# Two transformer blocks on one core: squares summed on GpSimd, a feed-forward that multiplies raw tokens, and first iterations walked by feature tile

## What is computed

```python
def rms_norm(x, g):
    y = xf * lax.rsqrt(jnp.mean(xf * xf, axis=-1, keepdims=True) + EPS)
    return y * g
def modulate(h, shift, scale):
    return h * (1.0 + scale) + shift
mod_x = silu(c) @ w_ada + b_ada                  # six vectors of 1024: shifts, scales, gates
x = x + gt_m * rms_norm(mix_x, g_post_mix)
fx = swiglu(modulate(rms_norm(x, g_pre_ffn), sh_f, sc_f), w_ffn_in, w_ffn_out)   # gu0, dn0
x = x + gt_f * rms_norm(fx, g_post_ffn)
...
h = h + 0.5 * swiglu_2(rmsnorm(h, ffn1_norm), w_gate, w_up, w_down)              # gu1, dn1
u = rmsnorm(h, mix_norm)                                                         # in2k, in2g, ...
h = h + mixed @ w_out                                                            # wout2
h = h + 0.5 * swiglu_2(rmsnorm(h, ffn2_norm), w_gate, w_up, w_down)              # gu2, dn2
return rmsnorm(h, final_norm)
```

## Time and profile before

| | |
|---|---|
| median of 3 runs | 1073.89 us (1072.05 to 1074.85) |
| profiled execution: its own time | 1075.8 us |
| profiled execution: span | 1074.0 us |
| mean granted TensorE clock | 0.97 |
| busy: TensorE, VectorE, ScalarE, GpSimd | 1016.3, 601.5, 529.1, 51.1 us |

### The profile page before, as it was taken

The page is one execution under the profiler, slowest core; times in us unless marked ns, Lnnn a source line. Parts: engine busy times, 40 slices in busy tenths (PEclk is TensorE's granted clock), DMA queues, the critical chain, the costliest instruction groups (busy, mean ns, idle before and its releaser), DMA issues.

```text
span 1074.0 us, 19630 instructions
## 1 busy us (share of the span) xinstructions
PE 1016.3 (95%) x7693; PEld 927.5 (86%) x7693; DVE 601.5 (56%) x902; ACT 529.1 (49%) x787; POOL 51.1 (5%) x73
## 2 busy tenths in 40 slices
PE   5788999997999999989999999999999999999996
PEld 0466566785999999979999999999888899999996
DVE  2643574657555554375555544665586766566653
ACT  3253345645555654355555433553554665655440
POOL 0021110001000000000000000200120000000000
PEclk9799999898999999989999999999899999999998
DMA  8676343134756587416556763653233356666741
GB/s 316 199 254 203 122 166 110 40 119 156 235 179 195 173 220 211 137 59 194 159 184 186 202 172 99 204 160 115 65 114 120 129 184 183 188 187 200 214 142 39
DMA packets 189438, 175.39 MB, mean 163 GB/s; under 512 B 7344, under 2 KB 178624, under 8 KB 189008
## 3 DMA queue, kind: packets, MB, share of 16 engines
q1 hardware_dynamic: 183744, 153.24, 46.7%
q0 software_dynamic: 4928, 17.51, 4.8%
q10 hardware_dynamic: 720, 4.02, 1.0%
HBM read 173.67 MB, written 1.05 MB: 163 GB/s over the span
## 4 chain that ended last, share of the span: by engine, by line
PE 87%; DVE 4%; DMA 4%; ACT 2%; issue 1%; POOL 0%; DVEq 0%; SPq 0%; ACTq 0%
PE acc L1695 23%; PE acc L1696 23%; PE acc L1697 23%; PE wk L1739 2%; DMA raw<-in_w_ada 2%; DMA stage<-in_w_ada 2%; PE acc L2039 2%; PE wk L2085 1%; PE wk L1766 1%; PE acc L1846 1%; PE acc L1848 1%; PE acc L1847 1%; PE wk L1911 1%; PE wk L2278 1%; PE wk L1897 1%
## 5 line engine op out<-in xcount | busy, mean ns | idle before, releaser
L993 DVE TENSOR_TENSOR lo<-raw,hi 128x1024 fp32r<-128x1024 f32 (+1 forms) x260 | 330.0, 1285 | 252.7 <-ACT hi L509 252.3
L1695 PE MATMUL acc<-nH,hi 128*128 128x256 f32 (+2 forms) x1400 | 402.1, 287 | 4.9 <-DVE nL L1390 3.7
L1696 PE MATMUL acc<-nL,hi 128*128 128x256 f32 (+2 forms) x1400 | 397.4, 284 | 0.0
L1697 PE MATMUL acc<-nH,lo 128*128 128x256 f32 (+2 forms) x1400 | 396.4, 283 | 0.0
L509 ACT ACTIVATE hi<-raw 128x1024 fp32r<-128x1024 f32 (+1 forms) x260 | 281.0, 1097 | 143.6 <-PE acc L1697 127.3
L1695 PEld LDWEIGHTS acc<-nH,hi 128*128 128x128 f32 (+1 forms) x1400 | 265.4, 190 | 9.1 <-issue 5.5
L1696 PEld LDWEIGHTS acc<-nL,hi 128*128 128x128 f32 (+1 forms) x1400 | 264.8, 189 | 0.9
L1697 PEld LDWEIGHTS acc<-nH,lo 128*128 128x128 f32 (+1 forms) x1400 | 264.9, 189 | 0.2
L1695 PE MATMUL acc<-gH,hi 128*128 128x256 f32 (+1 forms) x528 | 149.4, 283 | 0.0
L1697 PE MATMUL acc<-gH,lo 128*128 128x256 f32 (+1 forms) x528 | 149.2, 283 | 0.0
L1696 PE MATMUL acc<-gL,hi 128*128 128x256 f32 (+1 forms) x528 | 149.0, 282 | 0.0
(11 more groups left out here) (350 smaller groups left out, 1216.4 us busy)
## 6 DMA issues: line engine op xcount, KB each, us to landing
raw<-in_w_in SPq DMA_DIRECT2D x52, 512.0 KB, 3.6
...
```

Source lines behind the costliest of these rows:

```text
L993: dve.tensor_tensor(lo[:, j, 0:width], raw[:, j, 0:width], hi[:, j, 0:width].bitcast(F32), ALU.subtract).then_inc(lo_ready, 1)
L1695: pe.matmul(out_, wH, xH, start=start, stop=False)
L1696: pe.matmul(out_, wH, xL, start=False, stop=False)
L1697: return pe.matmul(out_, wL, xH, start=False, stop=stop)
```

## The change

- GpSimd adds the squares of feature tiles 0 to 6 in place (`square_sums`: six chained additions a norm); TensorE multiplies the sum and tile 7 with ones, two matmuls in place of eight (`sum_squares`, L1766 and L1768 of the new file).
- gu0 multiplies raw tokens times their gain (nH and nL come from R), as gu1 and gu2 do. Two more columns of nH and nL hold the shift vector, so its product with the weights falls out as columns T and T+1; `gate_up_shifted` multiplies by 1/rms and adds that column. gu0's four slabs are split while wout still runs, and the last copy out of wout comes behind the root.
- The first iteration of gu0, gu1 and gu2 goes by feature tile: for k = 0 to 5 both halves, then half 0 of k = 6 and 7, then the sum of squares, then half 1 of k = 6 and 7 (`gate_up` with `joint`).
- ada_half(12), (13) and (14) stand behind iterations 0, 3 and 6 of gu0, (15) behind its last; both turns behind the second iteration of dn0.
- The sum of norm 5 stands between the two slabs of in2k's first, narrow product.

```diff
+            def square_sums(n, width):
+                nonlocal links
+                pool.wait_ge(*squared(n, 0))
+                for k in range(1, KD - 1):
+                    pool.wait_ge(*squared(n, k))
+                    ins = pool.tensor_tensor(sq[:, 0, 0:width], sq[:, 0, 0:width], sq[:, k, 0:width], ALU.add)
+                    if k < KD - 2:
+                        links += 1
+                        ins.then_inc(pool_chain, 1)
+                        pool.wait_ge(pool_chain, links)
+                ins.then_inc(sq_sum, 1)
...
+            square_sums(1, T)
             pool.wait_ge(mm_done, 4 * BASE["gu0"])
-            for n in range(12, 16):
+            stage_half(12)
+            square_sums(2, T)
+            for n in range(13, 16):
                 stage_half(n)
+            square_sums(3, T)
+            square_sums(4, TM)
+            square_sums(5, TM)
             pool.wait_ge(mm_done, 4 * BASE["in2k"] + 4)
...
                     multiplied("dn0", i, j)
-                    copy_square(acc[:, j - 1:j, 0:T], ds(2 * i + j // 2, 1), j // 2)
+                    k = ds(2 * i + j // 2, 1)
+                    act.activation(sq[:, k, 0:T], acc[:, j - 1:j, 0:T], ACT.Square).then_inc(dn0_sq, 1)
+                    act.activation(Y[:, k, :], acc[:, j - 1:j, 0:T], ACT.Copy).then_inc(acc_free[j // 2], 1)
...
+            act.activation(nH[:, :, T:T + 2], mods[:, 24:32, 0:1].broadcast_to([P, KD, 2]), ACT.Copy).then_inc(nh_ready, 1)
             for j in range(4):
                 act.wait_ge(mm_done, 4 * (BASE["wout"] + 1) + j + 1)
-                copy_square(acc[:, j, :].rearrange("p (m t) -> p m t", m=2), slice(2 * j, 2 * j + 2), j // 2)
+                out_ = acc[:, j, :].rearrange("p (m t) -> p m t", m=2)
+                act.activation(sq[:, 2 * j:2 * j + 2, 0:T], out_, ACT.Square).then_inc(wout_sq, 1)
+                if j < 3:
+                    act.activation(Y[:, 2 * j:2 * j + 2, :], out_, ACT.Copy).then_inc(acc_free[j // 2], 1)
+                split(BASE["gu0"], j, 1024, ring_lead(BASE["gu0"]))
             norm_rms(1, T)
+            act.activation(Y[:, 6:8, :], out_, ACT.Copy).then_inc(acc_free[1], 1)
             for k in range(KD):
+                upper(gmod[:, k, 2:3], k, T, META, (r_ready, k + 1))
                 square_r(k, T, META, (r_ready, k + 1))
-                if k in (2, 7):
-                    split(BASE["gu0"], k // 7, 1024, ring_lead(BASE["gu0"]))
             norm_rms(2, T)
...
+            def gate_up_shifted(name, ahead):
                 def evac(i, j):
+                    if j == 1:
+                        multiplied(name, i, j)
+                        dve.tensor_copy(bcol[:, 0:2, :], acc[:, 0:2, T:T + 1])
+                        dve.tensor_tensor(sg[:, :, 0:T], acc[:, 0:2, 0:T], tokens_inv(T), ALU.mult).then_inc(acc_free[0], 1)
                     if j == 3:
                         multiplied(name, i, j)
-                        dve.wait_ge(acc_free[0], USE[name] + i + 1)
+                        dve.tensor_copy(bcol[:, 2:4, :], acc[:, 2:4, T:T + 1])
                         dve.wait_ge(lo_ready, 4 * (BASE[name] + i) + 5)
-                        dve.tensor_tensor(hbuf[:, :, 0:width], sg[:, :, 0:width], acc[:, 2:4, 0:width],
-                                          ALU.mult).then_inc(acc_free[1], 1)
-                        dve.wait_ge(gh_ready, COUNT[name] * f + i + 1)
-                        dve.tensor_tensor(gL[:, ds(2 * i, 2), 0:width], hbuf[:, :, 0:width],
-                                          gH[:, ds(2 * i, 2), 0:width].bitcast(F32), ALU.subtract).then_inc(gl_ready, 1)
+                        dve.tensor_tensor(hbuf[:, :, 0:T], acc[:, 2:4, 0:T], tokens_inv(T), ALU.mult).then_inc(acc_free[1], 1)
+                        dve.wait_ge(acc_free[1], USE[name] + i + 1)
+                        dve.wait_ge(sg_ready, i + 1)
+                        for m in range(2):
+                            ins = dve.scalar_tensor_tensor(out=hbuf[:, m, 0:T], in0=hbuf[:, m, 0:T], scalar=bcol[:, 2 + m, :],
+                                                           in1=sg[:, m, 0:T], op0=ALU.add, op1=ALU.mult)
+                        ins.then_inc(hb_ready, 1)
...
+            def sum_squares(n, width):
+                pe.wait_ge(sq_sum, n)
+                pe.matmul(wk[:, 0, 0:width], ones, sq[:, 0, 0:width], start=True, stop=False)
+                pe.wait_ge(*squared(n, KD - 1))
+                pe.matmul(wk[:, 0, 0:width], ones, sq[:, KD - 1, 0:width], start=False, stop=True).then_inc(ssq_ps, 1)
...
+            def gate_up(name, t0, width, behind=lambda: None, cuts=(), joint=None):
                 xs = (lambda k: nH[:, k, t0:t0 + width], lambda k: nL[:, k, t0:t0 + width])
-                for s in range(2):
-                    pair(BASE[name], USE[name], s, *xs, width, None if s else (nl_ready, first, 1), None if s else beside)
-                    if after:
-                        after[s]()
-                with pe.Fori(1, COUNT[name]) as i:
+                if joint is not None:
+                    for s in range(2):
+                        set_free(s, USE[name])
+                    g = BASE[name]
+                    steps = [(k, s) for k in range(KD - 2) for s in range(2)] + [(6, 0), (7, 0), (6, 1), (7, 1)]
+                    for k, s in steps:
+                        arrived(g, 2 + k // 4)
+                        pe.wait_ge(nl_ready, joint + k + 1)
+                        if (k, s) == (6, 1):
+                            behind()
+                        for m in range(2):
+                            j, w = 2 * s + k // 4, slice(256 * (k % 4) + P * m, 256 * (k % 4) + P * m + P)
+                            ins = split_mm(acc[:, 2 * s + m, 0:width], hi[:, j, w], lo[:, j, w], xs[0](k), xs[1](k),
+                                           k == 0, k == KD - 1)
+                            if (k, s) == (7, 1) and m == 0:
+                                ins.then_inc(mm_done, 1)
+                        if (k, s) in ((3, 0), (7, 0), (7, 1)):
+                            ins.then_inc(mm_done, 1)
+                else:
+                    pair(BASE[name], USE[name], 0, *xs, width)
+                    behind()
+                    pair(BASE[name], USE[name], 1, *xs, width)
+                first = 1
...
+            def last_turns():
+                ada_turn(6)
+                ada_turn(7)
+            sum_squares(1, T)
+            gate_up("gu0", 0, T + 2, lambda: sum_squares(2, T),
+                    ((1, lambda: ada_half(12)), (4, lambda: ada_half(13)), (7, lambda: ada_half(14))), 17)
             ada_half(15)
-            down("dn0", 0, T)
-            ada_turn(7)
-            sum_squares(sq, T, lambda k: (acc_free[k % 2], USE["dn0"] + k // 2 + 1))
-            def square_behind(k):
-                pe.wait_ge(sq_ready, 16 + k + 1)
-                sum_square(k, sq, TM)
-            gate_up("gu1", 24, 0, TM, square_behind)
+            down("dn0", 0, T, last_turns)
+            sum_squares(3, T)
+            gate_up("gu1", 0, TM, lambda: sum_squares(4, TM), (), 25)
             down("dn1", 1, TM)
-            sum_squares(sq, TM, lambda k: (sq_ready, 24 + k + 1))
...
-                    pe.wait_ge(nl_ready, 32 + k + 1)
+                    pe.wait_ge(nl_ready, 33 + k + 1)
                     ins = split_mm(acc[0:16, 0, 0:TM], hi[:, q, w], lo[:, q, w], nH[:, k, :], nL[:, k, :], k == 0, k == KD - 1)
                 ins.then_inc(mm_done, 1)
+                if q == 0:
+                    sum_squares(5, TM)
             pair(g, USE["in2k"], 1, *allT, TM)
...
-            gate_up("gu2", 40, 0, T)
+            gate_up("gu2", 0, T, lambda: sum_squares(6, T), (), 41)
```

More of the change, by code:

```diff
@@ L969, in _ @@
             for k in range(KD):
-                upper(N_F2, k, T, META, (acc_free[1], USE["gu2"]))
+                upper(gain(N_F2, k), k, T, META, (acc_free[1], USE["gu2"]))
             split(BASE["gu2"], 3, 1024, ring_lead(BASE["gu2"]))
@@ L1461, in evac_half, with modulated @@
                 return evac
-            post_norm(1, 3)
-            for j in (0, 1):
+            dve.wait_ge(nh_ready, 17)
+            dve.tensor_tensor(nL[:, :, T:T + 2], mods[:, 24:32, 0:1].broadcast_to([P, KD, 2]), nH[:, :, T:T + 2].bitcast(F32),
+                              ALU.subtract).then_inc(nl_ready, 1)
+            for j in range(4):
                 split(BASE["gu0"], j, 1024)
-            split_norm(2, 16, T, META, lambda k: gmod[:, k, 2:3], 24, BASE["gu0"])
+            def modulated(k):
+                if k >= 1:
+                    scaled_lower(17, k - 1, T, META, gmod[:, k - 1, 2:3])
+            post_norm(1, 3, modulated)
+            scaled_lower(17, KD - 1, T, META, gmod[:, KD - 1, 2:3])
+            norm_inv(2, T)
+            gate_up_shifted("gu0", DN)
+            pipeline("dn0", SLOT, nothing, K4[0:3] + [None], True)
             ada_columns(6)
-            gate_up("gu0", 0, T, DN)
-            pipeline("dn0", SLOT, nothing, K4[0:3] + [None], True)
```

(40 more changed lines are left out.)

102 lines of the change are left out of this document (41 added, 61 removed).

## The result

| | before | changed |
|---|---|---|
| median | 1074.30 us (4 runs, 1072.05 to 1074.85) | 1093.86 us (4 runs, 1092.01 to 1095.83) |
| profiled execution: its own time, span | 1075.8, 1074.0 us | 1092.01, 1090.2 us |
| mean granted clock | 0.97 | 0.96 |

The ratio is 1.0186, with a 95% interval of 1.0161 to 1.0211: 19.6 us slower, where 10.3 were forecast, and 1.9 us above the upper end of the range. The sign and the three new waits were right; two stretches of the sum were far too small. (Medians are over all executions; single ones of 5047.62 us in `e1_halves` and of 2492.88 us beside the last three experiments stand far off, and the ratios leave them out.)

A forecast was written before the change was run, and what follows sets the result against it. TensorE, 87% of the chain, was taken as the bound, issuing without gaps in long loops, leaving the six joints between stages to win. Terms summed to +10.3 us on 1073.9, about 1084 us; range 1070 to 1092.

The forecast's parts named there:

- The sign: Whole kernel: the change makes it slower, given a chance of 0.72.
- the three new waits: TensorE gaps of 3 to 5 us, released by VectorE's `sg`, ahead of the second iterations of gu0, gu1, gu2.
- wout to gu0's first matmul, -10.4: Between wout and gu0: first matmul near 251.9 in place of 262.3, 10.4 us earlier.
- gu0's first iteration, gu2's, and the waits of 3.8, 4.6, 4.7: First iterations: gu0 +3.8 us, gu2 +7.3; TensorE idles 3.8, 4.6, 4.7 us ahead of gu0's, gu1's, gu2's second iterations.
- The evacuation grows ... Zero, with up to 0.5 an iteration at the upper end: gu0's loop: added copies and operations cost nothing, since ScalarE and VectorE need about 10.5 us of an 11.3 us iteration.
- Two columns of 258: ... +1.0: gu0's loop: two more columns in each of 1056 matmuls cost 1.0 us, interpolated between 256 and 272 columns.
- GpSimd beside VectorE, "I take +1.0": gu1's first iteration: additions meeting VectorE cost 1.0 us, from slab splits 0.3 us longer; between 0 and 2.
- The rival built on the rule: gu1 and gu0: each addition stops VectorE for its whole 1.0 us, 8.5 us more, 1092.5 us; chance 0.10.
- Slab 3 in gu1, +2.7: gu1's first iteration: tile k = 4 must await slab 3's split, 9.15 us in; 20.7 us in place of 18.0.
- The clock, +1.7 a fall: Behind five new TensorE gaps: the granted clock falls, 1.7 us lost each time, 8.5 us in all.
- dn0 and its norm, -1.7: dn0 to gu1: two turns interrupting dn0 cost +1.6 us, the earlier reciprocal gives -3.3.
- From gu1's second iteration to gu2's first matmul, +2.7: This stretch gets 2.7 us longer, with clock falls of 1.7 us counted behind gu1's gap and at in2k.

The follow-up runs named there:

- e1_halves: Changed kernel with the first iterations of gu0, gu1, gu2 back in the order half 0, sum of squares, half 1: 1076.61 us, ratio 1.0015.
- the last three experiments: Unread matmuls filling TensorE's waits in a kernel combining the fixes (1066.95 us) and in the changed kernel (1091.84 us); mixed gu0 matmul widths in the changed kernel (1095.95 us).
- e10_filled: Changed kernel with unread matmuls filling TensorE's waits ahead of the second iterations of gu0, gu1 and gu2: 1091.84 us, ratio 1.0174.
- e11_widths: Changed kernel with plain evacuation in gu0 and its iterations 256, 260 or 264 columns wide: 1095.95 us, one execution.
- e5_both: Changed kernel with gu0's matmuls 256 columns wide and gu1's and gu2's plain evacuation in gu0, shift left out: 1091.10 us, ratio 1.0139.
- e2_no_adds: Changed kernel with five of GpSimd's six additions left out in each of norms 2 (gu0) and 4 (gu1): 1089.77 us, ratio 1.0146.

## Why the prediction was wrong, step by step

The miss of 9.1 us is 4.5 in gu0's loop and 4.1 in gu1's first iteration.

- *wout to gu0's first matmul, -10.4*: right. Of the 11.9 measured, 1.5 are chance: the clock fell behind a wait of 2.10 us in the profiled execution before and not in this one. An addition took 0.74 us behind wout (1.0 in the sum).
- *gu0's first iteration, gu2's, and the waits of 3.8, 4.6, 4.7*: right to 0.4 us, and shown by `e1_halves` to be the cause of most of the loss.
- *"The evacuation grows ... Zero, with up to 0.5 an iteration at the upper end"*: **this step failed**. The loop of ScalarE and VectorE was put at "about 10.5 us of an iteration of 11.3". Its lap without the new operations is 10.85 (gu2's distance from `sg` to `sg` in `e10_filled`, in the laps in which the two engines catch up with TensorE); two copies (0.15), one more product with its hand-over (0.9) and Silu in two parts (0.3) stand one behind another in it and make 12.2. The prediction names the copies and the added product; what it had wrong is that they would overlap with the rest, while all of them lie on one closed chain through both engines. The lap should have been added up from one `sg` to the next.
- *"Two columns of 258: ... +1.0"*: mis-sized. It was interpolated between 256 and 272, where `e11_widths` shows a step: 1056 x 0.0039 = 4.1. The lap of 12.17 hides most of it and is hidden by it: from gu0's second iteration to dn0 either limit alone costs 3.5 to 3.7 us (122.2 and 121.9 against 118.5) and both cost 4.2. What `e5_both` keeps is also dearer than the sum had it, 5.0 us in place of 3.7: each half of ada takes 1.2 us, and the granted clock is 0.53 over the first six microseconds.
- *GpSimd beside VectorE, "I take +1.0"*: mis-sized, on a row that did not carry over. That row is an operation with one input. An addition has two, and each costs VectorE 0.5 us, 2.7 us of the path in gu1. Whether the number of inputs makes the difference no run here tests. The Trainium skill's rule (SBUF — State Buffer, section on the two separate sides), by which "the other fully blocks", was set aside for that row. For additions this trace nearly agrees with it: in dn0 one that starts 0.39 us behind the start of a split of 1.63 takes 1.83 in place of 0.74, so it stood still for all but some 0.15 us of the rest of the split:

```profile
406.25 1.63 DVE L1019 TENSOR_TENSOR lo<-raw,hi 128x1408 fp32r<-128x1408 f32 x1 [1.98 <-ACT hi L540]
```

```profile
406.64 1.83 POOL L491 TENSOR_TENSOR sq<-sq 128x256 f32<-128x256 f32 x1 [64.24 <-ACT sq L788]
```

The rival built on the rule (8.5 us, with 1.0 for each addition) asked too much: an addition takes 0.77 us, VectorE loses 0.5 of it, and gu0 did not move at all in `e2_no_adds`. That the measured 1093.9 lies next to this rival's 1092.5 is chance.
- *Slab 3 in gu1, +2.7*: the place was right, but the wait that it makes (4.0 us) lowers the clock as the others do, and this fall was not counted: the 36 matmuls behind it take 7.0 us in place of 4.5. The sum priced every other new wait at 1.7 for the clock and never sized this one, which by its own numbers (9.15 + 1.0, less 48 matmuls of 6.0 to 7.7 us) comes out at 2.5 to 4.2 us. `e2_no_adds` takes both back: the wait is 1.29 us, no fall. With the 2.7 us of the additions in place of 1.0 this makes 4.2, the miss of this stretch.
- *The clock, +1.7 a fall*: 2.2 in gu1 and 1.4 in gu2 by `e10_filled`, and 0.3 in gu0. The evidence on short waits was read too narrowly: the trace before also had a wait of 2.62 us, to 250.54, and behind it a granted clock of 0.59 and 0.56 (252 to 254 and 254 to 256 us).
- *dn0 and its norm, -1.7*: within 0.5 us. *From gu1's second iteration to gu2's first matmul, +2.7*: 1.4 more, 0.5 of it gu1's clock; the rest is open. *The end*: right.
- *The range*: its upper end of 1092 lay below the forecast's own rival at 1092.5.
